# Second mixing layer: two head pairs scored between the last input product chunks, the forget product in three fp32r passes, the last norms among the attention steps

## The reference, cut to what matters

```python
def mix_forget_dilated(xn, w_in, b_f, g_q_c, g_k_c, g_q_d, g_k_d, cos, sin):
    proj = xn @ w_in                                  # 1024 -> 3*1024 + 8
    q, k, v = jnp.split(proj[..., :3 * D_MIX], 3, axis=-1)
    ...
    log_f = jax.nn.log_sigmoid((proj[..., 3 * D_MIX:] + b_f).astype(jnp.float32)).transpose(0, 2, 1)
    q_c = rms_norm(q[:, :H_C], g_q_c)                 # 8 "forget" heads: norm, no rotation
    k_c = rms_norm(k[:, :H_C], g_k_c)
    out_c = forgetting_attention(q_c, k_c, v[:, :H_C], log_f)
    q_d = apply_rope(rms_norm(q[:, H_C:], g_q_d), cos, sin)   # 8 "dilated" heads
    k_d = apply_rope(rms_norm(k[:, H_C:], g_k_d), cos, sin)
    out_d = dilated_window_attention(q_d, k_d, v[:, H_C:])
```

## Time and profile before

| | us |
|---|---|
| three runs, median | 2325.92 |
| three runs, lowest to highest | 2320.02 to 2329.15 |
| the profiled execution, its device time | 2310.36 |
| its span, first to last instruction | 2308.6 |

### The profile page before, as it was taken

The page is one execution under the profiler, slowest core; times in us unless marked ns, Lnnn a source line. Parts: engine busy times, 40 slices in busy tenths (PEclk is TensorE's granted clock), DMA queues, the critical chain, the costliest instruction groups (busy, mean ns, idle before and its releaser), DMA issues.

```text
span 2308.6 us, 35231 instructions
## 1 busy us (share of the span) xinstructions
PE 2049.0 (89%) x14104; PEld 1658.0 (72%) x14104; DVE 1273.9 (55%) x2329; ACT 805.8 (35%) x1335; POOL 638.0 (28%) x671
## 2 busy tenths in 40 slices
PE   7999989999999999999988999996768766776877
PEld 7999969999999978999977898774334322333435
DVE  5555635555655543555655444357656656666653
ACT  5444344444443442444455232212122122211222
POOL 0000010000000100000000232017777777777772
PEclk9999999999999987999999998998989997999989
DMA  9653506654564511755404110459999999999994
GB/s 306 200 182 115 177 11 212 198 182 146 185 198 146 169 51 37 234 172 179 129 19 146 38 39 21 132 180 371 380 384 378 364 368 375 362 366 373 393 408 156
DMA packets 254878, 489.60 MB, mean 212 GB/s; under 512 B 13936, under 2 KB 174224, under 8 KB 254624
## 3 DMA queue, kind: packets, MB, share of 16 engines
q0 software_dynamic: 73888, 268.53, 30.6%
q1 hardware_dynamic: 177104, 214.32, 28.5%
q10 hardware_dynamic: 3760, 5.02, 0.7%
HBM read 486.74 MB, written 1.05 MB: 211 GB/s over the span
## 4 chain that ended last, share of the span: by engine, by line
PE 69%; POOL 12%; DMA 6%; issue 5%; DVE 5%; ACT 3%; POOLq 0%; DVEq 0%; ACTq 0%
PE bank L757 68%; POOL arena_sb L2693 10%; DMA arena_sb<-peer_u,arena_sb 3%; POOL con_sb L2693 3%; DMA con_sb<-peer_v,arena_sb 2%; DMA arena_sb<-peer_v,arena_sb 1%; PE bank L908 1%; DVE parts_sb L2012 0%; DVE sq_sb L2565 0%; DVE xT_sb L2076 0%; DVE parts_sb L2007 0%; DMA xT_sb<-xT 0%; ACT parts_sb L1544 0%; DVE arena_sb L2412 0%; DMA ring_sb<-ffn_w_gate 0%
## 5 line engine op out<-in xcount | busy, mean ns | idle before, releaser
L757 PE MATMUL bank<-arena_sb 64*64 64x64 f32 (+7 forms) x3688 | 533.8, 332 | 151.8 <-ACT arena_sb L1963 113.3
L757 PE MATMUL bank<-xh_sb,parts_sb 128*128 128x256 f32 x3328 | 604.8, 284 | 19.8 <-DVE parts_sb L2007 16.4
L757 PEld LDWEIGHTS bank<-arena_sb 64*64 64x64 f32 (+4 forms) x3688 | 316.5, 168 | 359.8 <-issue 216.1
L757 PEld LDWEIGHTS bank<-xh_sb,parts_sb 128*128 128x128 f32 x3328 | 514.5, 190 | 26.2 <-issue 25.3
L757 PE MATMUL bank<-xl_sb,parts_sb 128*128 128x256 f32 x1808 | 510.0, 282 | 0.0
L2565 DVE CUSTOM_DVE_ANT_0 sq_sb<-arena_sb 128x1024 f32<-128x1024 f32 x256 | 309.6, 1224 | 251.4 <-DMA arena_sb<-peer_u,arena_sb 245.8
L2007 DVE TENSOR_TENSOR parts_sb<-ring_sb,parts_sb 128x2048 fp32r<-128x2048 f32 x132 | 298.7, 2290 | 174.9 <-ACT parts_sb L1530 174.9
L757 PEld LDWEIGHTS bank<-xl_sb,parts_sb 128*128 128x128 f32 x1808 | 343.6, 190 | 0.0
L2693 POOL DMA_INDIRECT arena_sb<-peer_u,arena_sb x256 | 281.8, 1101 | 196.5 <-DVE arena_sb L2513 112.3
L1530 ACT ACTIVATE parts_sb<-ring_sb 128x2048 fp32r<-128x2048 f32 x132 | 248.0, 1909 | 60.2 <-PE bank L757 58.9
L757 PE MATMUL bank<-h_high_sb,parts_sb 128*128 128x256 f32 x1408 | 255.9, 283 | 0.0
(11 more groups left out here) (269 smaller groups left out, 1877.2 us busy)
## 6 DMA issues: line engine op xcount, KB each, us to landing
ring_sb<-ffn_w_gate SPq DMA_DIRECT2D x44, 1024.0 KB, 5.4
ring_sb<-ffn_w_up SPq DMA_DIRECT2D x44, 1024.0 KB, 6.5
ring_sb<-ffn_w_down SPq DMA_DIRECT2D x44, 1024.0 KB, 4.9
ring_sb<-w_in SPq DMA_DIRECT2D x17, 1024.0 KB, 6.0
ring_sb<-w_in_ab SPq DMA_DIRECT2D x12, 1024.0 KB, 5.3
ring_sb<-w_out SPq DMA_DIRECT2D x12, 1024.0 KB, 5.2
ring_sb<-w_in_cd SPq DMA_DIRECT2D x12, 1024.0 KB, 5.4
ring_sb<-peer_w_q SPq DMA_DIRECT2D x8, 1024.0 KB, 5.3
```

The lines of the kernel that those rows point to most:

```text
L757: return pe.matmul(dst, lhsT, rhs, start=start, stop=stop_, skip_group_check=loose)
```

## The change

Four things, all in the second layer:

1. The forget product is split as the other weights are: ACT makes `WFH`, DVE makes `WFL` at the start of the layer, and PE does 24 fp32r matmuls (`mm3`) after slot 8 in place of 16 float32 ones after slot 11. The log-sigmoid on ACT moves to slot 10, the running sum on DVE behind the first `soft_max`.
2. The scores of head pairs 0 and 1 (of the step count, heads of pairs 4 and 5) are issued by PE after the second chunk of slot 10 and after the first chunk of slot 11. `soft_max`, `soft_exp` and the first transposes of these pairs move along with them, on DVE, ACT and PE.
3. The last two norms (`hssq` 6 and 7, `roots`, `normalise`) move among the attention steps: `hssq` 6 behind the first transposes, `hssq` 7 in step 2.
4. `hssq` 5, 6 and 7 and the forget product use bank 7, and the loop `soft(1, 8)` starts at t = 2 on all three engines.

```diff
+        WFH, WFL = fast("wf_high", [P, KC, 8], arena_at + 4 * 21568), fast("wf_low", [P, KC, 8], arena_at + 4 * 21632)
...
-            return [i for i in ([s - 5] if s < 11 else [6, 7]) if 0 <= i < n]
+            return [i for i in ([s - 5] if s < 11 else [6, 7] if l == 0 else []) if 0 <= i < n]
...
-                for t in range(n + 4):
+                for t in range(2 if l == 1 else 0, n + 4):
...
-                    if 2 <= t < n + 2:
+                    if l == 1 and t == 2:
+                        head_norm(1, 7)
+                    elif 2 <= t < n + 2:
                         soft_turned(l, t - 2)
...
                         fill_end(ins, label)
+                        if l == 1 and (s, half) in ((10, 1), (11, 0)):
+                            pe.wait_ge(S("rope_ready"), 7)
+                            soft_scores(1, s - 10)
...
+                    if l == 1 and s == 8:
+                        b = fill_begin(pe, ("forget", 1))
+                        pe.wait_ge(S("wf_split"), 1)
+                        for kk in range(KC):
+                            ins = mm3(b[0:8, 0:T], WFH[:, kk, :], WFL[:, kk, :], xh[:, kk, :], xl[:, kk, :], kk == 0, kk == KC - 1)[1]
+                        fill_end(ins, ("forget", 1))
                 if l == 1:
-                    b = fill_begin(pe, ("forget", 1))
-                    pe.wait_ge(S("wf_loaded"), 16)
-                    for kk in range(KC):
-                        ins = mm(b[0:8, 0:T], WF[:, kk, :], xh[:, kk, :].bitcast(F32), kk == 0, False)
-                        if kk == 0:
-                            release(ins)
-                        ins = mm(b[0:8, 0:T], WF[:, kk, :], xl[:, kk, :].bitcast(F32), False, kk == KC - 1)
-                    fill_end(ins, ("forget", 1))
+                    soft_turned(1, 0)
+                    head_norm(1, 6)
...
+                    if l == 1 and s == 10:
+                        emptied(act, ("forget", 1))
+                        ...
+                    if l == 1 and s == 11:
+                        soft_exp(1, 1)
...
+                    if l == 1 and s == 10:
+                        soft_exp(1, 0)
+                    if l == 1 and s == 11:
+                        soft_out(1, 0)
...
+                    soft(1, 8, {2: lambda: roots(7)})
...
+                if l == 1:
+                    dve.wait_ge(S("wf_high"), 1)
+                    dve.tensor_tensor(WFL[:, :, :], WF, WFH[:, :, :], ALU.subtract).then_inc(S("wf_split"), 1)
...
+                    if l == 1 and s == 9:
+                        b = take(dve, ("forget", 1))
+                        give(dve.tensor_tensor(FG[0:8, 2, :], b[0:8, 0:T], rstd[0:8, :], ALU.mult), ("forget", 1))
...
+                            if l == 1 and (s, m) in ((10, 9), (11, 10)):
+                                soft_max(1, s - 10)
+                                if s == 10:
+                                    forget()
...
+                    soft(1, 8, {2: lambda: normalise(6), 3: lambda: normalise(7)})
```

More of the change, by code:

```diff
@@ L403, in plan_layer @@
                     plan(label, 4 + (2 * s + j) % 3)
+                    if l == 1 and (s, j) in ((10, 1), (11, 0)):
+                        for e in range(2):
+                            plan(("s", l, s - 10, e), 2 * (s - 10) + e)
                 for i in norms_at(l, s):
-                    plan(("hssq", l, i), i % 2)
+                    plan(("hssq", l, i), 7 if (l, i) == (1, 5) else i % 2)
                 for i in turns_at(s):
                     plan(("rot", l, i), 2 + i % 2)
-            if l == 1:
-                plan(("forget", l), 7)
+                if l == 1 and s == 8:
+                    plan(("forget", l), 7)
             if l == 0:
@@ L424, in plan_layer @@
             else:
+                for i in (6, 7):
+                    plan(("hssq", l, i), 7)
                 plan_soft(l, 8)
@@ L431, in plan_soft @@
                 for e in range(2):
-                    if t < n:
+                    if t < n and (l, t) not in ((1, 0), (1, 1)):
                         plan(("s", l, t, e), 2 * (t % 2) + e)
@@ L955, in soft, with head_norm @@
                         soft_mixed(l, t - 4)
+            def head_norm(l, i):
+                b = fill_begin(pe, ("hssq", l, i))
+                pe.wait_ge(S("hsq_ready"), 4 * l + i + 1)
+                fill_end(mm(b[:, 0:512], C("heads", P), HSQ[i % 2], True, True), ("hssq", l, i))
             def stick_scores(p):
@@ L1037, in layer @@
                     for i in norms_at(l, s):
[L1038 to L1041, removed]
+                        head_norm(l, i)
                     for i in turns_at(s):
@@ L1638, in soft @@
             def soft(l, n, between={}):
-                for t in range(n + 2):
+                for t in range(2 if l == 1 else 0, n + 2):
                     if t < n:
                         soft_exp(l, t)
-                    if t >= 2:
+                    if t >= 2 and (l, t) != (1, 2):
                         soft_out(l, t - 2)
@@ L1687, in layer @@
                         high_qkv(l, s + 3)
+                    if l == 1 and s == 10:
+                        emptied(act, ("forget", 1))
+                        act.wait_ge(S("bf_loaded"), 16)
+                        chain.link(act, act.activation(FG[0:8, 0, :], FG[0:8, 2, :], ACT.Abs, bias=small[0:8, 40:41]))
+                        chain.link(act, act.activation(FG[0:8, 0, :], FG[0:8, 0, :], ACT.Exp, scale=-1.0))
+                        act.activation(FG[0:8, 0, :], FG[0:8, 0, :], ACT.Ln, bias=C("one", 1)[0:8, :]).then_inc(S("fln_ready"), 1)
+                    if l == 1 and s == 11:
+                        soft_exp(1, 1)
                     if 0 <= s - 4 < n:
@@ L2125, in soft @@
             def soft(l, n, between={}):
-                for t in range(n + 5):
+                for t in range(2 if l == 1 else 0, n + 5):
                     if t < n:
```

34 lines of the change are left out of this document (13 added, 21 removed).

## The result

The changed kernel takes **2289.06 us** (median of four runs, 2282.55 to 2297.99) against 2323.83 for the kernel before (four runs). The ratio is 0.9862, 95% interval 0.9834 to 0.9889, which is 26 to 39 us less. The forecast was 2297.0 us. In a second comparison, with six runs, it took 2297.52 us, ratio 0.9895 (0.9868 to 0.9922), 18 to 31 us less. The change makes the kernel faster; 26 to 31 us lies in both intervals.

The account below looks back on a forecast made before the run. PE was taken to bound the stage, by its work, four waits and above all a clock lost in them. Gains of 10.1 + 17.6 + 1.2 = 28.9 us gave 2297.0 us, range 2288 to 2317.

Parts of the forecast that it names:

- The clock: Second layer's attention: PE at 2.4 GHz when the loop begins and staying there; the loop's gain 17.6 us.
- Rival A: Second layer's attention loop: the clock falls anyway, leaving a gain of 10.1 us, 2315.8 us in total; chance 0.16.
- The loop: From pair 4's scores, 36.5 us at half clock become 18.9 at full clock, steps about 4.1 us; gain 17.6.
- the stage: From the two 512-column products behind slot 8 to the out product's first matmul: 28.9 us shorter.
- The front: From the end of slot 8 to pair 4's scores: 34.0 us all told, gain 10.1.
- The narrow product: Forget product after slot 8: 24 passes in 2.8 us instead of 7.0, saving 4.2, at least 1.8.
- Bank 3: PE's wait before pair 1's scores, for the bank `turn` 3 uses: 0.5 us, the largest wait.
- Rival B: Before pair 1's scores: DVE 3 us late, the clock falls there, 5.4 us slower, 2331 us; chance 0.05.
- Rival C: Attention loop at full clock becomes latency-bound, 1 us more a step, 5 less gain, 2302 us; chance 0.09.
- The total: Whole kernel: 28.9 us taken from the median of before, later stretches unchanged, giving 2297.0 us; chance 0.70.

Follow-up runs that it names:

- float32 forget early: Changed kernel with the forget product back in 16 float32 matmuls, still after slot 8: 2299.76 us, ratio 0.9888 to the kernel before.
- before filled: Kernel before, with five useless 512-column float32 products put into three PE waits: 2305.75 us, ratio 0.9926 to the kernel before.
- norms back: Changed kernel with the last two norms back behind slot 11: 2299.75 us, ratio 0.9908 to the kernel before.
- more filled: Changed kernel with useless products at three other PE waits (layer 0's attention, behind last block's attention): 2289.96 us, ratio 0.9867 to the kernel before.
- clock lost: Changed kernel with PE held before pair 4's scores until six POOL memsets have run (the hold, 3.78 us idle): 2309.48 us, ratio 0.9941 to the kernel before.
- forget alone: Kernel before with only the forget product in 24 fp32r passes, still after slot 11: 2319.85 us, ratio 0.9989 to the kernel before.

## Why the prediction was right

**The clock, its largest term.** It was forecast at 1.00 from 815 to past 890. It was, in both executions. Taking the clock from the new order costs 15 us beside the hold, giving it to the old order brings 18.9. The support that the forecast had for it was thinner than it said: its first stretch at 1.00, the other layer's attention, was read up to 327.0, and the trace of before has 0.50 from 328 to 338 in the same attention, behind waits of PE. Rival A (the clock falls in the loop anyway) is refuted for this loop: it has eight transposes in each step and depth-2 products, and the clock held through it in five kernels (changed, float32 forget early, before filled, norms back, more filled). The Trainium skill ("TensorE: Matmul & The Clock Gate", Part 4) has transposes not count as PE-busy; this loop, in which 0.71 of 4.43 us are the six transposes (856.48 to 857.19), was granted full clock throughout, so that rule did not decide here.

**The loop, the term that was mis-sized.** I took 18.9 us between bounds of 18.2 and 20.8; it is 20.34, and a step is 4.43, not 4.1. That makes 1.4 of the 1.8 us that the stage lacks; the wait of 0.31 at its end is 0.3 of it. The forecast's reason was that "scores and transposes stream long rows" and would halve. The pieces, at half clock (from the run with the clock lost) and at full:

| piece of a step | half, us | full, us | ratio |
|---|---|---|---|
| 16 scores | 3.77 | 2.11 | 0.56 |
| 6 transposes | 1.33 | 0.71 | 0.53 |
| 12 values | 2.46 | 1.29 | 0.52 |
| 2 on the mixed rows | 0.56 | 0.32 | 0.57 |

It was the other way round. The values halve almost; of the three large pieces the scores, which I took to halve, do so least. The ratio of 1.40/2.46 that I gave the values came from a row that stood behind an idle piece of 0.51; in the loop the same twelve take 1.29.

**The front** came out at 34.15 against 34.0, but by two errors that cancel. The waits are 0.42 us where I had 1.55: DVE and ACT were in time for pair 0 and all but in time for the rest. PE's work is 33.73 where I had 32.45. About half of the difference is that a pair's scores were priced net of the tail: they cost 0.85 (833.44 to 834.29 in PE's timeline) and not 0.7, four times over. Most of the rest stands where PE runs into a wait or goes from one kind of product to another: the chunk behind pair 0's scores, with the two sums ahead of it, took 4.83 us and not 4.55, the next one 2.95 and not 2.8, and `hssq` 6 and 7 took 0.96 and 1.05 and not 0.87. The narrow product is no part of it: with the two sums ahead of it, it takes 4.47 (815.80 to 820.27) where the prices give 4.55, and its passes start 0.114 apart. (Its first pass is recorded with 0.52, but the two sums ahead with 1.32 in place of 1.75; a chunk behind two such sums is recorded in the same way.) Two slips of the working did no harm: 98 passes in 11.3 us are 0.115 for one and not 0.118, but the chunks of slot 9 after have 48 in 5.68, which is 0.118; and the terms of the front add up to 33.8 and not 34.0. Bank 3 was the largest wait, as forecast, with 0.22. Rival B needed DVE 3 us late; it was 0.22. On DVE the softmax of pair 0 begins at 834.39, and the instruction that frees bank 3 (L2205), behind sum and norm, ends at 839.19; the forecast's queue had that order:

```profile
834.39 0.29 DVE L2127 CUSTOM_DVE_ANT_0 arena_sb<-bank,con_sb 128x128 f32<-128x128 f32 x1 [0.42 <-PE bank L763]
...
838.51 0.68 DVE L2205 TENSOR_TENSOR arena_sb<-bank,con_sb 128x512 f32<-128x512 f32 x1
```

**Rival C** (the loop becomes bound by latency) is refuted: in a step of 4.43 us PE is busy 4.43, while DVE and ACT have 2.15 and 2.25:

```profile
854.37:858.80 4.43, 4.43 (x38) 3.35 (x37) 2.15 (x12) 2.25 (x7) 0.00 (x0) 1.00 0.00 0
```

**The total.** The forecast took 28.9 us from the median of before and left the rest unchanged. The first comparison gave 32 us less, the second 24; the forecast lies between them and inside both intervals, and so do the stage's 27.1. What moves between equal kernels lies outside the stage: 2.1 us ahead of it in the two profiles of the changed kernel (it starts at 815.80 and at 813.74), and more behind it. The first gather and the last one, from POOL's timeline, before and then after:

```profile
1540.36 1.04 POOL L2693 DMA_INDIRECT arena_sb<-peer_u,arena_sb  x1 [112.29 <-DVE arena_sb L2513]
...
2269.47 0.94 POOL L2693 DMA_INDIRECT con_sb<-peer_v,arena_sb  x1 [0.30 <-issue]
```
```profile
1511.25 1.04 POOL L2720 DMA_INDIRECT arena_sb<-peer_u,arena_sb  x1 [113.00 <-DVE arena_sb L2540]
...
2255.56 1.04 POOL L2720 DMA_INDIRECT con_sb<-peer_v,arena_sb  x1 [0.30 <-issue]
```

At the first gather the changed kernel is 29.1 us ahead, at the last 13.9: in this execution the same gathers took 744.3 us instead of 729.1. In the second profile of the changed kernel it is 23.8 ahead at the first, and the gathers take 741.1. Among the nine profiled executions the gathers lie between 729 and 744 us, though none of the kernels touches them. So a single span tells nothing of a change of this size.

The stretch between the stage and the first gather varies too, and there the trace says why. PE in the changed kernel, first and second profile:

```profile
876.14:1511.25 635.11, 607.45 (x5826) 0.97 0.35 111
```
```profile
874.09:1516.54 642.45, 614.79 (x5826) 0.95 0.34 110
```

PE idles 27.66 us in both; the 7.3 us of difference are busy time of the same 5826 instructions, of which 41 us are at half clock in the one and 58 in the other. In all nine profiles this stretch takes 635 to 651 us with 41 to 71 us at half clock, the longer the more. Before has 638.8 us with 48, so the first profile of the changed kernel gained 3.7 us there and the second lost 3.7, neither by the change. The forecast took this stretch as unchanged; on the average of the two profiles it was. Why the runs of the first comparison came out at 32 and those of the second at 24 stays open, since only one run of each has a profile.

What decides whether the clock falls is open too. In the second layer it fell with pieces of 0.47, 0.72, 1.71 and 1.71 us and behind one of 3.78; it held through 0.47 and 2.54. And the order of the code does not settle it: in layer 0's attention, which the change does not touch, the same wait of 2.93 us stands in both profiles of the changed kernel. In the first the scores behind it run at half clock (0.50 from 305 to 308, which with a second fall at 328 makes the 8 in slice 6), in the second at full clock:

```profile
305.37 2.93 PE L763 MATMUL bank<-arena_sb 64*128 64x128 f32 x16 [2.93 <-ACT arena_sb L1650]
```
```profile
304.45 1.58 PE L763 MATMUL bank<-arena_sb 64*128 64x128 f32 x16 [2.93 <-ACT arena_sb L1650]
```

So a fall or a hold that is seen in one profile could have come out otherwise in another execution. For the second layer's loop there are nine profiles. In the three with the old waits or the hold in place the clock fell, in the six others it held, once (norms back) with a wait of 2.54 us ahead of it.

## What to carry to other kernels

Look at the granted clock beside the idle time of PE: four waits of 4.6 us in all cost another 19 us here, since the loop behind them ran at half clock. Real work moved into such waits is best, and where there is none, products of constants into a free bank bring most of it. Saving PE time ahead of a stretch at half clock may bring nothing: 4.3 us saved alone were gone at the end of the out product. And compare the time at half clock outside the stage before a difference of a few us is put down to a change.

## What the runs showed of the hardware

- A loop that keeps PE busy does not bring the clock back soon: it ran at half clock for 44.4 us with PE busy 42.8 of them (before), 54 with 52.9 (forget alone) and 35 with 35.0 (clock lost) before full clock was granted.
- The same wait of 2.93 us at the same place of the code brought the clock down in one execution (305.37) and not in another (304.45).
- Halving the clock does not double the time of small products: 16 scores take 3.77 us against 2.11.
- Three fp32r passes with eight output columns take 0.34 us (3 x 0.114), where the two float32 matmuls that they replace take 0.87 (7.0 us for 16).
